# Cross-attention's output projection in two halves of 512 columns, first query groups on token tiles 0 to 3, on one Trainium2 core

## The chip, the cores and the metric

The kernel runs on one core of one Trainium2 chip. The metric is the device time in microseconds (us). The kernel before the change takes 2323.01 us, the median of three runs (2319.06 to 2325.57).

## What is computed

One encoder layer on 1024 tokens of width 1024, all in float32. The reference, cut to the parts that the change lies in:

```python
x = x + concat(A, B) @ W_out              # mixing block, ends just ahead of the change
h = rms_norm(x, norm_xattn_g)
q = (h @ wq)                              # 1024 x 1024, 4 heads of 256
s = q k^T * XATTN_DH ** -0.5              # 256 memory tokens
o = softmax(s) v
x = x + o @ wo                            # output projection
h = rms_norm(x, norm_ffn_g)
logits = h @ router_w + router_b          # 32 experts
top_vals, top_idx = lax.top_k(logits, 4)  # then 4 of 32 experts per token, clamped SwiGLU
```

## The kernel before the change

Tokens lie in 8 tiles of 128 rows, and each 1024-wide contraction in 8 slices of 128. Every engine has its own stream of instructions, written out by hand in order; an engine takes its stream strictly in order, and a semaphore wait at the head of a stream holds all that stands behind it. PE is the matrix engine, DVE the vector engine, ACT the scalar engine, POOL the general one, SP the one that issues most DMAs.

A float32 product is made of three fast products: each operand is split into a high part (a rounded copy, made by ACT) and a low part (the rest, made by DVE by subtraction), and PE adds high x high, high x low and low x high. So each weight chunk of 256 columns, which SP loads into the four-slot buffer `ring`, needs one ACT copy of 128x2048 (`split_wq`, `split_wo`) and one DVE subtraction of 128x2048 (`wq_lo`, `wo_lo`) before PE can use it.

The stages around the change, in order of time:

- **Norm y and query projection (q).** `y_square`, `y_root` (ACT), `y_mean`, `y_scale` (DVE) norm one token tile; `turn_y` (PE) transposes it by eight small matmuls; `hidden_states_hi` (ACT) and `hidden_states_lo` (DVE) split it into `hH` and `hL`. Then 16 groups of 24 matmuls, each 512 tokens wide (tiles 0 to 3, or 4 to 7), four groups for each weight chunk. `turn_y(5)` stands ahead of group 0, `turn_y(6)` ahead of group 1, `turn_y(7)` ahead of group 2.
- **Softmax loop.** 32 steps (4 heads x 8 token tiles) in which PE, DVE and ACT hand each tile on: `score` (PE), `scale_maximum` (DVE), `xprob` (ACT, exponential), `normalise` (DVE), `turn_probabilities` (PE), `xprob_drain` (ACT). From step 10 on, four steps out of eight also hold `head_values` (PE), `xout_hi` (ACT) and `xout_lo` (DVE).
- **Output projection (o).** 32 groups of 24 matmuls, each 256 columns wide: for each of four weight chunks all eight token tiles. DVE adds each group into `xres` (`add_residual`). `woH` and `woL` are two-deep buffers.
- **Norm z and router.** As soon as the last chunk's group of a tile is added, the tile is normed (`z_square`, `z_mean`, `z_root`, `z_scale`), stored, transposed (`turn_z`, PE, 8 small matmuls), copied out (`h3_turned_out`, ACT, two copies). For each pair of tiles `router` (PE) makes partial logits, `logits_out` (ACT) copies them, `sum_groups` (PE) adds the groups up, and DVE takes the best four of 32 (`logits`, `one_hot`). The routing tables follow, then the loop over experts, some three fifths of the time.

Of the kernel before, what the change touches and what calls it, by code (L numbers as in the profile page):

```python
# [25 lines left out]
P = 128  # L26
S = 1024
D = 1024
# [38 lines left out]
def build(nc, A):  # L67

    with ExitStack() as ctx:
# [68 lines left out]
        woH = [sb(f"woH{i}", [P, KT, 256], FR, 96 + 16 * i) for i in range(2)]  # L138
        woL = [sb(f"woL{i}", [P, KT, 256], FR, 104 + 16 * i) for i in range(2)]
# [27 lines left out]
        h3 = sb("h3", [P, TT, D], F, 0)  # L167
# [82 lines left out]
        for n in ("m", "x", "y", "z"):  # L250
# [67 lines left out]

        chunks = ([(w_in, G0), (w_in, A0), (w_in, B0), (w_in, A0 + 256), (w_in, B0 + 256),
# [3 lines left out]
                  + [(wo, 256 * c) for c in range(4)])  # L323
# [3 lines left out]
                + [("out", 8 * (c + 1)) for c in range(4)] + [("q", 4 * (c + 1)) for c in range(4)]  # L327
                + [("o", 8 * (c + 1)) for c in range(4)])
# [93 lines left out]
        def o_bank(n):  # L422
            return PS[:, n % 8 if n < 3 * TT else n % 2, 0:256]
# [38 lines left out]
        def _(sp):  # L462
# [51 lines left out]
            for t in range(TT):  # L514
                sp.wait_ge(norms["z"]["scaled"], t + 1)
                sp.dma_start(h3_dram[P * t:P * (t + 1), :], h3[:, t, :]).then_inc(s_h3s, 16)
# [271 lines left out]
        def _(act):  # L788
# [325 lines left out]
            def split_wq(c):  # L1114

                act.wait_ge(s_ring[slot_of[g_q + c]], 16 * fills[g_q + c])
                if c == 1:
                    act.wait_ge(s_mm["out"], 4 * TT)
                if c >= 2:
                    act.wait_ge(s_mm["q"], 4 * (c - 1))  # L1120
                nc.scalar.copy(wqH[c % 2][:], ring[:, slot_of[g_q + c]]).then_inc(s_dhi, 1)
# [32 lines left out]
            for t in range(TT - 4, TT):  # L1154
                hidden_states_hi(t)
            split_wq(1)
            for n in range(16):
                d = drain("q", n)
                c, ft, th = q_group(n)
                nc.scalar.copy(qxT[:, 2 * c + ft, 512 * th:512 * (th + 1)], bank_groups(n)).then_inc(d, 1)  # L1160
                if n in (3, 7):
                    split_wq(n // 4 + 2)
# [9 lines left out]
            def split_wo(c):  # L1172

                act.wait_ge(s_ring[slot_of[g_o + c]], 16 * fills[g_o + c])
                if c >= 2:
                    act.wait_ge(s_mm["o"], TT * (c - 1))
                nc.scalar.copy(woH[c % 2][:], ring[:, slot_of[g_o + c]]).then_inc(s_dhi, 1)
# [21 lines left out]
            split_wo(1)  # L1199
# [12 lines left out]
            def z_square(t):  # L1212
                act.wait_ge(s_dr["o"], 24 + t + 1)
                if t:
                    act.wait_ge(NZ["stats_by_scalar"], square_of(t - 1))
                nc.scalar.activation(sig[:], xres[:, t, :], ACT.Square,
                                     accum_out=st8[:, 0, t:t + 1]).then_inc(NZ["stats_by_scalar"], 1)

            def z_root(t):
                act.wait_ge(NZ["stats_by_vector"], square_of(t))  # L1220
                nc.scalar.activation(st8[:, 2, t:t + 1], st8[:, 1, t:t + 1], ACT.Sqrt
                                     ).then_inc(NZ["stats_by_scalar"], 1)
# [15 lines left out]
            z_square(0)  # L1238
# [8 lines left out]
            z_root(TT - 1)  # L1247
            h3_turned_out(4)
            logits_out(1)
            h3_turned_out(5)  # L1250
            h3_turned_out(6)
            logits_out(2)
            h3_turned_out(7)
# [239 lines left out]
        def _(dve):  # L1493
# [404 lines left out]
            for c in range(1, 4):  # L1898
                wq_lo(c)
            def wo_lo(c):  # L1900

                dve.wait_ge(s_dhi, N_IN + 8 + c + 1)
                nc.vector.tensor_tensor(woL[c % 2][:], ring[:, slot_of[len(chunks) - 4 + c]], woH[c % 2][:].bitcast(F),
                                        ALU.subtract).then_inc(s_dlv, 1)
# [34 lines left out]
            wo_lo(1)  # L1939
            for n in range(3 * TT):  # L1940
                add_residual("o", n, o_bank)
                if n in (TT - 1, 2 * TT - 1):
                    wo_lo(n // TT + 2)
# [5 lines left out]
            def z_mean(t):  # L1949
                dve.wait_ge(NZ["stats_by_scalar"], square_of(t))  # L1950
                nc.vector.tensor_scalar(st8[:, 1, t:t + 1], st8[:, 0, t:t + 1], 1.0 / D, RMS_EPS, ALU.mult, ALU.add
                                        ).then_inc(NZ["stats_by_vector"], 1)

            def z_scale(t):
                dve.wait_ge(NZ["stats_by_scalar"], root_of(t))
                nc.vector.reciprocal(st8[:, 3, t:t + 1], st8[:, 2, t:t + 1]).then_inc(NZ["stats_by_vector"], 1)
                dve.wait_ge(NZ["stats_by_vector"], root_of(t))
                nc.vector.scalar_tensor_tensor(out=h3[:, t, :], in0=xres[:, t, :], scalar=st8[:, 3, t:t + 1],
                                               in1=gfb[:], op0=ALU.mult, op1=ALU.mult).then_inc(NZ["scaled"], 1)
# [24 lines left out]
            for t in range(TT + 8):  # L1984
                if t < TT:
                    add_residual("o", 3 * TT + t, o_bank)
                if 1 <= t <= TT:
                    z_mean(t - 1)
                if 2 <= t <= TT + 1:
                    z_scale(t - 2)  # L1990
                if 7 <= t <= TT + 6:
                    logits(t - 7)
                if t >= 8:
                    one_hot(t - 8)
# [351 lines left out]
        def _(pe):  # L2346
# [336 lines left out]
            turn_y(5)  # L2683
            pe.wait_ge(NY["drained"], TT)
            for c in range(4):
                pe.wait_ge(s_dlv, c + 1)
                slot = slot_of[g]
                for i in range(4):
                    n = 4 * c + i
                    _, ft, th = q_group(n)  # L2690
                    if n in (1, 2):
                        turn_y(5 + n)
                    if n == 2:
                        pe.wait_ge(NY["drained"], 2 * TT)
                    if n >= 8:
                        pe.wait_ge(s_dr["q"], n - 7)
                    w, rows = slice(P * ft, P * (ft + 1)), slice(512 * th, 512 * (th + 1))
                    for k in range(KT):
                        wh, wl = wqH[c % 2][:, k, w], ringL[:, slot, k, w]
                        xh, xl = hH[:, k, rows], low_of(k)[:, rows]  # L2700
                        pe.matmul(bank_groups(n), wh, xh, start=(k == 0), stop=False)  # L2701
                        pe.matmul(bank_groups(n), wh, xl, start=False, stop=False)
                        ins = pe.matmul(bank_groups(n), wl, xh, start=False, stop=(k == KT - 1))
                    ins.then_inc(s_mm["q"], 1)
                g += 1
# [39 lines left out]
            def turn_z(t):  # L2745
                pe.wait_ge(NZ["scaled"], t + 1)
                if t < 2:
                    pe.wait_ge(s_dr["o"], 3 * TT)
                else:
                    pe.wait_ge(s_h3e, 2 * (t - 1))  # L2750
                for b in range(2):
                    for k in range(4):
                        ins = pe.transpose(PS[:, 4 + 2 * (t % 2) + b, P * k:P * (k + 1)],
                                           h3[:, t, P * (4 * b + k):P * (4 * b + k + 1)], ident[:])
# [24 lines left out]
            for c in range(4):  # L2779
                pe.wait_ge(s_dlv, 4 + c + 1)  # L2780
                for t in range(TT):
                    n = TT * c + t
                    if n >= 8:
                        pe.wait_ge(s_dr["o"], n - 7 if n < 26 else n - 1)
                    tile = slice(P * t, P * (t + 1))
                    for k in range(KT):
# [4 lines left out]
                    if n >= 27:  # L2791
                        turn_z(n - 27)
                    if n == 29:
                        router(0)
                    elif n == 31:
                        sum_groups(0)
                        router(1)

            turn_z(5)
            sum_groups(1)  # L2800
            turn_z(6)
            router(2)
            turn_z(7)
            sum_groups(2)
            router(3)
            sum_groups(3)
            pe.wait_ge(s_dr["o"], 32)
# [212 lines left out]
```

## Time and profile before

| what | value |
|---|---|
| runs of the kernel before, median | 2323.01 us (2319.06, 2323.01, 2325.57) |
| span of the profiled execution | 2318.4 us |
| PE busy | 2181.9 us, 94% of the span |
| DVE busy | 1794.7 us, 77% |
| ACT busy | 1268.4 us, 55% |
| query projection, from PE's first to last matmul | 553.67 to 647.05 us |
| softmax loop | 647.88 to 728.25 us |
| output projection, PE | 728.31 to 825.4 us |
| end of router, first matmul of the routing tables | 843.92 us |
| first expert transposes | 893.99 us |

The profiled execution has no separate time beside its span of 2318.4 us; the fastest of the three runs is 0.7 us above that span and the median 4.6 us. Busy shares are averages over stages: PE is dense in the two projections and in the expert loop, and waits in the softmax loop and around the routing.

### The profile page before, as it was taken

To read this page: it belongs to the slowest core of one execution; us is meant where nothing else is said; L and a number is where in the kernel's file an instruction comes from. 1 tells how busy PE (TensorE), PEld (TensorE's weight loads), DVE (VectorE), ACT (ScalarE), POOL (GpSimd) and SP (SyncE) were. 2 spreads that over 40 slices of the span, in tenths; PEclk is the share of its full clock that TensorE was granted. 3 is DMA by queue.
4 is the path that set the end of the run, shared out by engine and by line. 5 is a ranking of instruction groups with operands and counts; after the bars stand their busy time and mean duration, and the time that the engine had idled before them with its cause. 6 is when DMAs were issued, how large, how long until landed. Compare 5 with 4: busy or idle time off the path is not lost.

```text
span 2318.4 us, 41683 instructions
## 1 busy us (share of the span) xinstructions
PE 2181.9 (94%) x14731; PEld 1742.5 (75%) x14865; DVE 1794.7 (77%) x2020; ACT 1268.4 (55%) x1437; POOL 358.8 (15%) x311
## 2 busy tenths in 40 slices
PE   5999998799989977999999999999999999999995
PEld 4789977698856956777877777777777777877773
DVE  5599989815043376899989898898998989998885
ACT  4422265604142145666766666666666666776554
POOL 0000000020002102222211221122122112221112
PEclk8899999999999988999999999999999999999997
DMA  4211141321101036989988798789788888997777
GB/s 156 72 38 55 37 148 38 125 68 37 55 19 33 10 133 241 385 307 343 402 296 315 292 343 291 278 332 350 295 325 303 300 296 346 397 342 307 278 260 249
DMA packets 113300, 515.58 MB, mean 222 GB/s; under 512 B 11424, under 2 KB 45397, under 8 KB 63714
## 3 DMA queue, kind: packets, MB, share of 16 engines
q1 hardware_dynamic: 97810, 467.28, 52.0%
q0 software_dynamic: 13504, 44.24, 7.9%
q10 hardware_dynamic: 1904, 2.90, 0.5%
q8 instruction: 60, 0.98, 0.2%
q14 instruction: 22, 0.18, 0.0%
HBM read 477.12 MB, written 37.36 MB: 222 GB/s over the span
## 4 chain that ended last, share of the span: by engine, by line
PE 75%; DVE 11%; issue 7%; DMA 4%; ACT 3%; DVEq 0%; POOLq 0%; ACTq 0%; POOL 0%; SPq 0%
PE PS L2901 14%; PE PS L2902 12%; PE PS L2375 10%; PE PS L2904 9%; PE PS L2928 5%; PE PS L2788 4%; PE PS L2630 4%; PE PS L2893 3%; PE PS L2864 2%; DVE wlo L2120 2%; PE PS L2916 1%; ACT whi L1289 1%; DMA raw<-in_exp_w_up 1%; PE PS L2732 1%; PE PS L2701 1%
## 5 line engine op out<-in xcount | busy, mean ns | idle before, releaser
L2120 DVE TENSOR_TENSOR wlo<-raw,whi 128x2048 fp32r<-128x2048 f32 x384 | 869.9, 2287 | 99.7 <-ACT whi L1289 88.9
L1289 ACT CAST whi<-raw 128x2048 fp32r<-128x2048 f32 x384 | 725.2, 1911 | 118.9 <-DMA raw<-in_exp_w_down 55.3
L2901 PE MATMUL PS<-whi,xhi 128*128 128x512 f32 x1024 | 424.2, 414 | 12.7 <-issue 9.3
L2902 PE MATMUL PS<-wlo,xhi 128*128 128x512 f32 x1024 | 400.4, 391 | 0.0
L2904 PE MATMUL PS<-whi,xlo 128*128 128x512 f32 x768 | 301.8, 393 | 0.0
L2902 PEld LDWEIGHTS PS<-wlo,xhi 128*128 128x128 f32 x1024 | 193.3, 189 | 39.9
L2901 PEld LDWEIGHTS PS<-whi,xhi 128*128 128x128 f32 x1024 | 194.2, 190 | 37.8 <-DVE wlo L2120 0.7
L2901 PE MATMUL PS<-whi,hhi 128*128 128x512 f32 x512 | 206.8, 404 | 8.7 <-DVE wlo L2120 5.3
L2902 PE MATMUL PS<-wlo,hhi 128*128 128x512 f32 x512 | 200.6, 392 | 0.0
L2904 PEld LDWEIGHTS PS<-whi,xlo 128*128 128x128 f32 x768 | 144.8, 189 | 31.9
L2904 PE MATMUL PS<-whi,hlo 128*128 128x512 f32 x384 | 150.7, 392 | 0.0
L696 POOL COPY idxc<-TG 128x2 uint32 (+1 forms) x34 | 31.8, 935 | 763.7 <-PE PS L2864 395.6
L1630 DVE SCALAR_TENSOR_TENSOR yT<-u_pad,CWT,yT 128x1024 f32<-128x1024 f32 x120 | 144.3, 1284 | 0.0
L729 POOL DMA_INDIRECT acc_scratch<-yb,idxs x64 | 139.3, 2176 | 22.8 <-issue 22.8
L1347 ACT ACTIVATE yb<-PS,row_gate 128x512 f32<-128x512 f32 x62 | 42.7, 688 | 153.1 <-PE PS L2928 83.5
L2901 PEld LDWEIGHTS PS<-whi,hhi 128*128 128x128 f32 x512 | 96.8, 189 | 39.0 <-issue 10.6
L1338 ACT ACTIVATE sgm<-glu 128x512 f32<-128x512 f32 (+1 forms) x64 | 53.4, 834 | 130.1 <-DVE glu L2165 76.1
L1847 DVE TENSOR_TENSOR xres<-xres,PS 128x256 f32<-128x256 f32 x64 | 26.5, 420 | 125.6 <-PE PS L2788 64.1
L706 POOL DMA_INDIRECT xs<-h_scratch,idxc x68 | 110.5, 1624 | 19.6 <-issue 17.6
L2902 PEld LDWEIGHTS PS<-wlo,hhi 128*128 128x128 f32 x512 | 97.0, 189 | 18.6
L2928 PE MATMUL PS<-raw,xtl 128*32 128x256 f32 x1664 | 103.7, 381 | 0.0
L2893 PE MATMUL PS<-whi,xlo 128*128 128x512 f32 x256 | 99.6, 389 | 0.0
(439 smaller groups left out, 4234.9 us busy)
## 6 DMA issues: line engine op xcount, KB each, us to landing
raw<-in_exp_w_up SPq DMA_DIRECT2D x256, 1024.0 KB, 8.0
raw<-in_exp_w_down SPq DMA_DIRECT2D x128, 1024.0 KB, 7.3
ring<-in_w_in SPq DMA_DIRECT2D x11, 1024.0 KB, 5.8
xres<-in_x SPq DMA_DIRECT2D x4, 1024.0 KB, 10.3
ring<-in_xattn_wk SPq DMA_DIRECT2D x4, 1024.0 KB, 9.2
ring<-in_xattn_wv SPq DMA_DIRECT2D x4, 1024.0 KB, 6.1
ring<-in_w_out SPq DMA_DIRECT2D x4, 1024.0 KB, 12.3
xres<-in_x SPq DMA_DIRECT2D x2, 2048.0 KB, 8.2
```

The lines of the kernel that those rows point to most:

```text
L706: nc.gpsimd.indirect_dma_start(xs[0:rows, b, :], None, h3_dram, bass.IndirectOffsetOnAxis(ap=idxc[0:rows, b:b + 1], axis=0)).then_inc(s_xs ...
L729: nc.gpsimd.indirect_dma_start(acc_dram, bass.IndirectOffsetOnAxis(ap=idxs[0:rows, b:b + 1], axis=0), yb[0:rows, b, :], None, compute_op=A ...
L1289: nc.scalar.copy(whi[:, chunk_slot(c, NSPL), :], raw[chunk_slot(c, NRAW)][:]).then_inc(s_whi, 1)
L1630: ins = nc.vector.scalar_tensor_tensor(out=yT[:, c, :], in0=uc, scalar=w, in1=yT[:, c, :], op0=ALU.mult, op1=ALU.add)
L2120: nc.vector.tensor_tensor(wlo[:, chunk_slot(c, NSPL), :], raw[chunk_slot(c, NRAW)][:], whi[:, chunk_slot(c, NSPL), :].bitcast(F), ALU.subtract
L2375: ins = pe.matmul(out, lhs, rhs, start=(k == 0 and i == 0), stop=(k == KT - 1 and i == 2))
L2630: ins = pe.matmul(out_bank(n), a, b, start=(k == 0 and i == 0 and n >= TT), stop=(k == KT - 1 and i == 2 and n >= TT))
L2893: return pe.matmul(o, lo[:, k, :], whi[:, slot, 3, :], start=False, stop=k == KT - 1)
L2901: pe.matmul(o, hi[:, k, :], wh, start=k == 0 and bias is None, stop=False)
L2902: pe.matmul(o, hi[:, k, :], wl, start=False, stop=False)
L2904: pe.matmul(o, lo[:, k, :], wh, start=False, stop=False)
L2928: ins = pe.matmul(part[2 * (k % 2) + h], tl[:, k, 0:TAIL], chunk[:, k % 4, cols[h]], start=k == 1 or k == 0 and bias is None, stop=k >= KT ...
```

## The change

The diff, cut to its core (SP's list of chunks, buffers, ACT, DVE, PE):

```diff
-        woH = [sb(f"woH{i}", [P, KT, 256], FR, 96 + 16 * i) for i in range(2)]
-        woL = [sb(f"woL{i}", [P, KT, 256], FR, 104 + 16 * i) for i in range(2)]
+        woP = sb("woP", [P, 4, KT, 256], FR, 96)
...
-        h3 = sb("h3", [P, TT, D], F, 0)
+        h3 = [sb("h3a", [P, 2, D], F, 0), sb("h3b", [P, 2, D], F, 24)]
...
+        WO_COLS = (1, 0, 2, 3)
...
         def q_group(n):
-            c, i = n // 4, n % 4
-            ft, th = (i % 2, i // 2) if c == 0 else (i // 2, i % 2)
-            return c, ft, th
+            if n < 8:
+                return n % 4 // 2, n % 2, n // 4
+            return n // 4, n % 4 // 2, n % 2
...
         def o_bank(n):
-            return PS[:, n % 8 if n < 3 * TT else n % 2, 0:256]
+            return PS[:, n if n < TT else n % 2, :]
...ACT, norm y and softmax loop
-            for t in range(TT - 4, TT):
+            hidden_states_hi(TT - 4)
+            split_wq(1)
+            for t in range(TT - 3, TT):
                 hidden_states_hi(t)
-            split_wq(1)
...
                 if 2 <= step < N_SC + 2:
                     xprob_drain(step - 2)
-            split_wo(1)
+                if step == TT:
+                    split_wo(1)
...ACT, norm z
-            for t in range(1, TT):
-                if t >= 4:
-                    h3_turned_out(t - 4)
+            for t in range(TT):
                 z_square(t)
-                z_root(t - 1)
-                if t == 6:
-                    logits_out(0)
+                z_root(t)
+                if t:
+                    h3_turned_out(t - 1)
+                if t in (3, 5, 7):
+                    logits_out((t - 3) // 2)
...DVE
                 if value_part(step - 1):
                     xout_lo(*value_part(step - 1))
-            wo_lo(1)
+                if step == TT:
+                    wo_lo(1)
+
+            def add_attention(n):
+                dve.wait_ge(s_mm["o"], n + 1)
+                xs = xres[:, n % TT, 512 * (n // TT):512 * (n // TT + 1)]
+                nc.vector.tensor_tensor(xs, xs, o_bank(n), ALU.add).then_inc(s_dr["o"], 1)
...
+            for t in range(TT):
+                add_attention(TT + t)
+                if t >= 4:
+                    one_hot(t - 4)
+                z_mean(t)
+                z_scale(t)
+                if t >= 3:
+                    logits(t - 3)
+            one_hot(4)
+            for t in range(5, TT):
+                logits(t)
+                one_hot(t)
...PE
             pe.wait_ge(s_dr["out"], 32)
-            turn_y(5)
             pe.wait_ge(NY["drained"], TT)
...
+                if n == 0:
+                    turn_y(5)
+                    turn_y(6)
+                if n == 1:
+                    turn_y(7)
...
+            for half in range(2):
+                pe.wait_ge(s_dlv, 4 + 2 * (half + 1))
...
                 for t in range(TT):
-                    n = TT * c + t
+                    n = TT * half + t
...
                     for k in range(KT):
-                        for i, (a, b) in enumerate(((oxH, woH), (oxH, woL), (oxL, woH))):
-                            ins = pe.matmul(o_bank(n), a[:, k, tile], b[c % 2][:, k, :],
+                        wh, wl = woP[:, wide, k, :], ringL[:, lows, k, :]
+                        for i, (a, b) in enumerate(((oxH, wh), (oxH, wl), (oxL, wh))):
+                            ins = pe.matmul(o, a[:, k, tile], b,
                                             start=(k == 0 and i == 0), stop=(k == KT - 1 and i == 2))
+                        if half and t in (3, 5, 7) and k == 3:
+                            router((t - 3) // 2)
                     ins.then_inc(s_mm["o"], 1)
...
+                    if half and t:
+                        turn_z(t - 1)
+                    if half and t in (3, 5, 7):
+                        sum_groups((t - 3) // 2)
+
+            turn_z(TT - 1)
             router(3)
             sum_groups(3)
```

What it does. The query projection's first four groups take both first weight chunks on tiles 0 to 3, so chunk 1 is split earlier and the transposes of tiles 5 to 7 stand behind groups 0 and 1. The output projection runs as 16 groups of 24 matmuls of 512 columns; each matmul's moving operand is two blocks of 256 columns that lie apart in memory. Chunks 0 and 1 must both be split ahead of its first group, and chunk 1's split moves into step 8 of the softmax loop. The add into `xres` is 512 wide. In the second half each tile is complete after its one group, and its norm, transpose and router work stand between the groups.

On PE, around the first group of the query projection, names as before (`XNy` is the normed tile, L2659 `turn_y`, L2701 to L2703 the three products). Before:

```order
L2659 MATMUL PS<-ident,XNy_105 128x128 x8
L2659 MATMUL PS<-ident,XNy_106 128x128 x8
L2701 MATMUL PS<-hH,wqH_107 128x512
L2702 MATMUL PS<-hL_102,wqH_107 128x512
L2703 MATMUL PS<-hH,ringL 128x512
```

After:

```order
L2672 MATMUL PS<-ident,XNy_105 128x128 x8
L2709 MATMUL PS<-hH,wqH_107 128x512
L2710 MATMUL PS<-hL_102,wqH_107 128x512
L2711 MATMUL PS<-hH,ringL 128x512
```

The second transpose (tile 5) no longer stands ahead of the first product; it comes 24 matmuls later, with that of tile 6 right behind it.

On ACT, steps 7 to 9 of the softmax loop (`pr` the probabilities, `pT` the transposed ones), after the change:

```order
L1190 ACTIVATE pr,smx<-PS,smx 128x256
L1175 COPY pT<-PS 128x2x128
L1183 CAST woP<-ring 128x2048
L1190 ACTIVATE pr,smx<-PS,smx 128x256
L1175 COPY pT<-PS 128x2x128
```

The CAST is `split_wo(1)`; before, it stood behind the whole loop, after the last `oxH`. DVE has the matching subtraction (`ringL<-ring,woP`) at the same step, behind `normalise(7)` and ahead of `scale_maximum(9)`.

On PE, the end of the fourth group of the second half (`h3b` the normed tile, L2766 `turn_z`, L2787 `sum_groups`, L2805 the projection), after the change:

```order
L2805 MATMUL PS<-ringL,oxH 128x512
L2805 MATMUL PS<-woP,oxL 128x512
L2766 MATMUL PS<-ident,h3b 128x128 x8
L2787 MATMUL PS<-stack,lgs 128x32 x2
L2805 MATMUL PS<-woP,oxH 128x512
```

and on ACT the rows of the same tile, the square and root of tile 3 first, then tile 2's two copies and the logits' copy that `sum_groups(0)` reads:

```order
L1223 ACTIVATE sig,st_120<-xres 128x1024
L1228 ACTIVATE st_120<-st_120 128x1
L1236 COPY h3T<-PS 128x512 x2
L1243 COPY lgs<-PS 128x256
```

Before, `sum_groups(0)` stood behind the last group of the projection, eight tiles on; now it stands three groups after the first tile is complete, and again so for the second and third pair.

## Rows read from the trace of the kernel before

**Rows 1.** The page, the chain that ended last, by engine.

```profile
PE 75%; DVE 11%; issue 7%; DMA 4%; ACT 3%; DVEq 0%; POOLq 0%; ACTq 0%; POOL 0%; SPq 0%
```

**Rows 2.** Timeline of PE, query projection (start, duration, instruction, [idle before]).

```profile
553.67 1.39 PE L2659 MATMUL PS<-ident,XNy 128*128 128x128 f32 x8 [2.45 <-DVE hL L1882]
...
570.74 0.50 PE L2701 MATMUL PS<-hH,wqH 128*128 128x512 f32 x1 [1.68 <-DVE hL L1882]
...
571.54 0.40 PE L2701 MATMUL PS<-hH,wqH 128*128 128x512 f32 x1
...
646.82 0.39 PE L2703 MATMUL PS<-hH,ringL 128*128 128x512 f32 x1
```

**Rows 3.** The chain that ended last, 545 to 560 us (start, time in chain).

```profile
557.19 0.43 PE PS L2703
...
557.93 0.23 PE PS L2702
```

**Rows 4.** Timeline of all engines, softmax steps 8 to 10.

```profile
664.53 0.36 ACT L1167 COPY pT<-PS 128x256 f32<-128x256 f32 x1
...
664.94 0.42 DVE L1928 TENSOR_REDUCE smx<-PS 128x1 f32<-128x256 f32 x1 [0.44 <-PE PS L2712]
...
665.28 1.03 PE L2712 MATMUL PS<-kx,qxT 128*128 128x256 f32 x4
...
666.47 1.98 PE L2732 MATMUL PS<-pT,vx 128*128 128x512 f32 x4 [0.15 <-ACT pT L1167]
```

**Rows 5.** Timeline, end of the softmax loop and first group of o.

```profile
727.43 1.90 ACT L1177 CAST woH<-ring 128x2048 fp32r<-128x2048 f32 x1
...
728.31 0.39 PE L2788 MATMUL PS<-woH,oxH 128*128 128x256 f32 x1 [1.40 <-DVE oxL L1910]
...
729.36 2.29 DVE L1903 TENSOR_TENSOR woL<-ring,woH 128x2048 fp32r<-128x2048 f32 x1 [1.11 <-ACT woH L1177]
```

**Rows 6.** The chain that ended last, groups of o with transposes and router between.

```profile
810.08 2.87 PE PS L2788 x24
812.95 0.87 PE PS L2753 x8
...
817.57 1.00 PE PS L2766 x16
818.57 3.07 PE PS L2788 x24
```

**Rows 7.** Timeline, norm z of the last tile and a sum of logits.

```profile
825.41 0.42 DVE L1847 TENSOR_TENSOR xres<-xres,PS 128x256 f32<-128x256 f32 x1 [1.86 <-PE PS L2788]
...
825.87 1.06 ACT L1216 ACTIVATE sig<-xres 128x1024 f32<-128x1024 f32 x1 [1.26 <-DVE xres L1847]
...
826.83 0.19 ACT L1216 ACTIVATION_READ_ACCUMULATOR sig<-xres 128x1 f32 x1
...
828.01 0.20 ACT L1221 ACTIVATE st<-st 128x1 f32<-128x1 f32 x1 [0.89 <-DVE st L1951]
...
829.49 0.63 PE L2774 MATMUL PS<-stack,lgs 128*128 128x32 f32 x4 [0.85 <-ACT lgs L1236]
```

**Rows 8.** Timeline, from the last transpose to the routing tables.

```profile
832.32 1.09 PE L2753 MATMUL PS<-ident,h 128*128 128x128 f32 x8 [0.29 <-DVE h L1958]
...
835.20 0.18 DVE L1964 TENSOR_TENSOR LG<-PS,rbb 128x32 f32<-128x32 f32 x1
...
835.70 0.63 PE L2774 MATMUL PS<-stack,lgs 128*128 128x32 f32 x4 [0.49 <-ACT lgs L1236]
...
836.71 0.18 DVE L1964 TENSOR_TENSOR LG<-PS,rbb 128x32 f32<-128x32 f32 x1
836.74 2.33 POOL L691 TENSOR_TENSOR bdn<-bdn,bdn 32x1024 fp32r<-32x1024 f32 x1 [73.30 <-ACT bdn L1257]
...
837.34 1.76 DVE L1972 CAST IXf<-IX 128x8 f32<-128x8 uint32 x1
...
843.92 0.21 PE L2813 MATMUL PS<-Mb,beforeb 128*128 128x32 bf16 x2 [7.59 <-issue]
```

More of the change, by code:

```diff
@@ L322, in build @@
                   + [(w_out, 256 * c) for c in range(4)] + [(wq, 256 * c) for c in range(4)]
-                  + [(wo, 256 * c) for c in range(4)])
+                  + [(wo, 256 * c) for c in WO_COLS])
         used = ([("in", n) for n in (2, 14, 18, 22, 26, 30, 34, 42, 50, 62, 70)]
                 + [("mem", 2 * (c + 1)) for c in range(8)]
-                + [("out", 8 * (c + 1)) for c in range(4)] + [("q", 4 * (c + 1)) for c in range(4)]
-                + [("o", 8 * (c + 1)) for c in range(4)])
+                + [("out", 8 * (c + 1)) for c in range(4)] + [("q", n) for n in (6, 8, 12, 16)]
+                + [("o", 8), ("o", 8), ("o", 16), ("o", 16)])
         N_IN, g_out = 11, 19
@@ L422, in o_bank, with z_square_count, z_root_count @@
         def o_bank(n):
-            return PS[:, n % 8 if n < 3 * TT else n % 2, 0:256]
+            return PS[:, n if n < TT else n % 2, :]
+        def z_square_count(t):
+            return 2 * t + 1
+        def z_root_count(t):
+            return 2 * t + 2
         GM, ZB, CB, LG_, LB, NG = 0, 8, 12, 16, 20, 24
@@ L1174, in split_wo @@
                 act.wait_ge(s_ring[slot_of[g_o + c]], 16 * fills[g_o + c])
-                if c >= 2:
-                    act.wait_ge(s_mm["o"], TT * (c - 1))
-                nc.scalar.copy(woH[c % 2][:], ring[:, slot_of[g_o + c]]).then_inc(s_dhi, 1)
+                nc.scalar.copy(woP[:, WO_COLS[c]], ring[:, slot_of[g_o + c]]).then_inc(s_dhi, 1)
             split_wo(0)
@@ L1897, in _ @@
                     hidden_states_lo(t - 4)
-            for c in range(1, 4):
+                if t == TT:
+                    wq_lo(1)
+            for c in range(2, 4):
                 wq_lo(c)
@@ L1938, in _ @@
                     xout_lo(*value_part(step - 1))
-            wo_lo(1)
[L1940 to L1943, printed above, removed]
+                if step == TT:
[4 more added lines that the diff above has]
+                nc.vector.tensor_tensor(xs, xs, o_bank(n), ALU.add).then_inc(s_dr["o"], 1)
+            for n in range(TT):
+                add_attention(n)
+                if n in (1, 3):
+                    wo_lo(n // 2 + 2)
             NZ = norms["z"]
@@ L1954, in z_scale @@
             def z_scale(t):
-                dve.wait_ge(NZ["stats_by_scalar"], root_of(t))
+                dve.wait_ge(NZ["stats_by_scalar"], z_root_count(t))
                 nc.vector.reciprocal(st8[:, 3, t:t + 1], st8[:, 2, t:t + 1]).then_inc(NZ["stats_by_vector"], 1)
-                dve.wait_ge(NZ["stats_by_vector"], root_of(t))
-                nc.vector.scalar_tensor_tensor(out=h3[:, t, :], in0=xres[:, t, :], scalar=st8[:, 3, t:t + 1],
+                dve.wait_ge(NZ["stats_by_vector"], z_root_count(t))
+                if t >= 4:
+                    dve.wait_ge(s_h3s, 16 * t)
+                    dve.wait_ge(NZ["turned"], 2 * (t - 3))
+                nc.vector.scalar_tensor_tensor(out=h3_of(t), in0=xres[:, t, :], scalar=st8[:, 3, t:t + 1],
                                                in1=gfb[:], op0=ALU.mult, op1=ALU.mult).then_inc(NZ["scaled"], 1)
@@ L1982, in one_hot @@
                                         ).then_inc(s_hot, 1)
[L1984 to L1994, printed above, removed]
+            for t in range(TT):
+                add_attention(TT + t)
+                if t >= 4:
+                    one_hot(t - 4)
[7 more added lines that the diff above has]
+                one_hot(t)
             dve.wait_ge(s_hot, 4 * TT)
@@ L2682, in _ @@
             pe.wait_ge(s_dr["out"], 32)
-            turn_y(5)
             pe.wait_ge(NY["drained"], TT)
-            for c in range(4):
+            for n in range(16):
+                c, ft, th = q_group(n)
                 pe.wait_ge(s_dlv, c + 1)
[L2687 to L2705, printed above, removed]
+                slot = slot_of[g + c]
+                if n == 4:
+                    pe.wait_ge(NY["drained"], 2 * TT)
+                if n >= 8:
+                    pe.wait_ge(s_dr["q"], n - 7)
+                w, rows = slice(P * ft, P * (ft + 1)), slice(512 * th, 512 * (th + 1))
+                for k in range(KT):
+                    wh, wl = wqH[c % 2][:, k, w], ringL[:, slot, k, w]
+                    xh, xl = hH[:, k, rows], low_of(k)[:, rows]
+                    pe.matmul(bank_groups(n), wh, xh, start=(k == 0), stop=False)
+                    pe.matmul(bank_groups(n), wh, xl, start=False, stop=False)
+                    ins = pe.matmul(bank_groups(n), wl, xh, start=False, stop=(k == KT - 1))
+                ins.then_inc(s_mm["q"], 1)
+                if n == 0:
[3 more added lines that the diff above has]
+                    turn_y(7)
+            g += 4
             pe.wait_ge(s_dr["q"], 16)
@@ L2747, in turn_z @@
                 if t < 2:
-                    pe.wait_ge(s_dr["o"], 3 * TT)
+                    pe.wait_ge(s_dr["o"], TT)
                 else:
@@ L2778, in _ @@
             pe.wait_ge(s_axl, 16)
-            for c in range(4):
-                pe.wait_ge(s_dlv, 4 + c + 1)
+            for half in range(2):
+                pe.wait_ge(s_dlv, 4 + 2 * (half + 1))
+                lows = slice(0, 4, 3) if half == 0 else slice(1, 3)
+                wide = slice(2 * half, 2 * half + 2)
                 for t in range(TT):
-                    n = TT * c + t
+                    n = TT * half + t
                     if n >= 8:
-                        pe.wait_ge(s_dr["o"], n - 7 if n < 26 else n - 1)
+                        pe.wait_ge(s_dr["o"], n - 7 if n < 10 else n - 1)
                     tile = slice(P * t, P * (t + 1))
+                    o = o_bank(n).rearrange("p (c n) -> p c n", c=2)
                     for k in range(KT):
-                        for i, (a, b) in enumerate(((oxH, woH), (oxH, woL), (oxL, woH))):
-                            ins = pe.matmul(o_bank(n), a[:, k, tile], b[c % 2][:, k, :],
+                        wh, wl = woP[:, wide, k, :], ringL[:, lows, k, :]
+                        for i, (a, b) in enumerate(((oxH, wh), (oxH, wl), (oxL, wh))):
+                            ins = pe.matmul(o, a[:, k, tile], b,
                                             start=(k == 0 and i == 0), stop=(k == KT - 1 and i == 2))
+                        if half and t in (3, 5, 7) and k == 3:
+                            router((t - 3) // 2)
                     ins.then_inc(s_mm["o"], 1)
[L2791 to L2804, printed above, removed]
+                    if half and t:
[3 more added lines that the diff above has]
+            turn_z(TT - 1)
             router(3)
             sum_groups(3)
-            pe.wait_ge(s_dr["o"], 32)
+            pe.wait_ge(s_dr["o"], 2 * TT)
             pe.wait_ge(s_hot, 4 * TT)
```

31 lines of the change are left out of this document (13 added, 18 removed).

## The prediction

> **What bounds the kernel now.** I read the chain of work that ended last first: three quarters of it is PE, a tenth DVE [rows 1]. The two projections that the change touches are PE from end to end, so there a matmul saved is time saved. Between them lies the softmax loop, in which each step passes through PE, DVE and ACT in turn, and behind them the router, where PE waits for ACT and DVE, and the chain runs through DVE's picks. Everything behind the router (routing tables, gather, expert loop) starts from its end, so a shift of that end is a shift of the whole. I read the timeline for four places and ask of each what waits last. Times are from the one profiled execution, span 2318.4 us; the sum is a difference, and I put it on the runs' median of 2323.0, which is 4.6 above that span.
>
> **Query projection.** Now PE waits twice: 2.45 us ahead of `turn_y(5)`, for tile 3's low part, and 1.68 us ahead of group 2, for tile 7's [rows 2]. The first wait stays: group 0 needs the same low part. The second goes, because groups 0 to 3 need tiles 0 to 3 only, and tile 7's low part, late by 1.7 us today, now has two more groups (11 us) to get ready. Chunk 1's split is one ACT copy of 1.9 and one DVE subtraction of 2.3 us, behind tile 4's copies; it is done some 6 us after PE starts, and group 2 asks for it at 15 us. It pushes tile 7's scaling by under 3 us, which `turn_y(7)` (14 us in) doesn't feel. The sum: 332 matmuls from 571.54 to 646.82 are 0.2267 us each [rows 2], so a group is 5.44. After the first wait PE's matmuls start 0.43 us apart up to 557.6 and 0.23 after it [rows 3]: the clock is at 1.2 GHz for some 3.7 us after PE stood idle for 2.45, and at 2.4 GHz after 1.68 idle. The stage is 384 x 0.2267 = 87.05, three transposes at 0.87 = 2.6, and about 1.7 of half clock = 91.4, against 93.4 now (553.67 to 646.82 + 0.23). **Minus 2.0 us.**
>
> **Softmax loop.** Today chunk 1's split runs 727.43 to 731.65, behind the loop, while PE already works on chunk 0 [rows 5]: it costs nothing. Now it stands in step 8. ACT does it after the copy that ends at 664.89 [rows 4], for 1.9 us; DVE can't begin before that copy is done, and stands still until then; it subtracts for 2.3 us. So `scale_maximum(9)`, at 664.94 today, starts at 664.8 + 1.93 + 2.2 = 668.95, 4.0 us late. Behind it on ACT are `xprob(9)` and `xprob_drain(7)`, and `head_values` (666.47 today) waits for that drain. PE can run ahead by score 10 only (ends 666.31 [rows 4]) and then stands idle some 4.2 us. Nothing gives this back: the steps that follow are PE's own. Bounds: 0 if the loop had slack, 4.2 if all of both instructions counts. I take 4.0. On top, 4.2 us idle is more than the 2.45 that halved the clock, and the next steps, with `head_values`, are bound by PE: some 3.5 us at half clock, as behind the first wait of the query projection [rows 3], lose 1.6. **Plus 5.6 us.**
>
> **Output projection up to its last group.** Two 256-wide matmuls take 2 x 2.87 / 24 = 0.239 us [rows 6], one 512-wide 0.2267 [rows 2]. The q groups read a moving operand in one piece; here it is two pieces of 256, which no row shows. Bounds: 0.2267 (no price) and 0.239 (all of the gain lost), 5 us apart over 384 matmuls. I take the low one, since the pieces are long. The Trainium skill, "TensorE: Matmul & The Clock Gate", section "Back-to-back issue gap", gives N/2.4 + 2.5 ns at full clock, by which pairs of 256 lose just 2.5 ns against a 512, 1.0 us in all where the rows give 5.0; the measured pitch of both shapes is above it, so the rows decide.
> From the first matmul (728.31) to where DVE can start on the last group: 97.1 today (825.41 [rows 7]). Then: 16 x 5.44 + 0.2 = 87.2; six `turn_z` at 0.87 = 5.2; three routers at 1.0 + 0.2 [rows 6] = 3.6; two `sum_groups` at 0.5 (each lasts 0.63 [rows 7], the next instruction starts a little before its end) = 1.0. That would be 97.0, no change. But the `sum_groups` wait. Let T be the moment DVE starts on tile 3. Its add is twice as wide as the 0.42 of today [rows 7]: between that and 0.84, I take 0.7. ACT's square starts at T + 0.73 and its sum is out 1.15 later (825.87 to 826.83 + 0.19 [rows 7]), T + 1.88; mean on DVE, 0.15 and two hand-overs, root starts T + 2.10. Only then come tile 2's two copies and the logits' copy, since ACT works in order: from root to PE's sum is 829.49 - 828.01 = 1.48 [rows 7], so T + 3.58. PE has finished issuing `turn_z(2)` at T + 0.65. It stands for **2.9 us**, and every later group is behind it. The same at the second pair: 5.9 in two. Its idle time by the record is 2.6 us each, above the 2.45 that halved the clock and well above the 1.68 that didn't: 1.6 each, 3.2. So 97.1 becomes 97.0 + 5.9 + 3.2 = 106.1. **Plus 9.0 us.** The new waits of `z_scale` for stored tiles cost nothing: a store lands 3 us after its issue and a group and a half lie between.
>
> **The tail.** Today 18.5 us from 825.41 to 843.92 [rows 7, 8]: four tiles of norm and all of the picks are still to do. After the change only tile 7's norm and four tiles' picks are. PE's third sum at T + 3.58, `turn_z(7)` at T + 4.1, the last sum 3.38 behind it (832.32 to 835.70 [rows 8]), T + 7.5, DVE's picks from T + 8.1. Picks for a tile are 1.51 (835.20 to 836.71 [rows 8]); two tiles hang on the last sum: T + 11.2. POOL's 2.33 us operation stops DVE's copy for 1.6 today (1.76 instead of 0.15 [rows 8]); it starts 1.04 after the last sum there and here, so it still hits: up to 1.9, T + 13.1. The third wait of 2.6 us leaves the transposes and the router at half clock: 1.0 more. 14.1 against 18.5. **Minus 4.4 us.**
>
> **Sum:** -2.0 + 5.6 + 9.0 - 4.4 = +8.2, and 2323.0 + 8.2 = 2331.
>
> **Rivals.** (0.3% is 7 us, about what a measurement of this kernel tells from no change.)
> (a) *The clock holds.* The short waits don't lower it: for it, 1.68 us idle did nothing; against it, 2.45 did. Then -3.2 in the projection, -1.0 in the tail, -1.6 in the softmax loop: 8.2 - 5.8 = +2.4, 2325, not slower by this measure. It decides from the point where two of the four drops fail to come.
> (b) *The two pieces cost.* A 512-wide matmul on two blocks goes at the pace of two 256-wide ones, or worse: +5, 2336. For it, no row has this shape; against it, each piece is 1 KB long. By the pitch that the Trainium skill gives, 4 us less would be saved than by my rows, near 2335.
> (c) *The logits' copy is not late.* If PE didn't wait for it, the projection would cost 97.0 and the tail 13.1: -2.0 + 5.6 - 0.1 - 5.4 = -1.9, 2321. Against it: ACT's order has the copy behind tile 3's root, and the root behind DVE's add of the very group that PE has just ended. It would take ACT records out of that order.
> (d) *The split in step 8 is hidden*, with the rest as forecast: +8.2 - 5.6 = +2.6, 2325.6. Against it, DVE and ACT wait for each other under 0.5 us a step [rows 4].
>
> **How the numbers follow.** Forecast (all four terms within 3 us in sum) 0.52; (a) 0.18; (b) 0.15; (c) 0.08; (d) 0.07. Of the forecast's own range, 2327 to 2335, some six tenths are above +7. So slower by over 0.3%: 0.52 x 0.62 + 0.15 + a little of (a) = 0.50; within it 0.39, from the rest of the forecast, (a), (d) and most of (c); faster 0.11, since the runs themselves differ by 6 us and the stages behind may fall differently. The range from (c) to beyond (b): 2321 to 2338.
>
> **What the profile after would show.** In the query projection one PE wait of some 2.5 us and none ahead of group 2. In step 9 of the softmax loop an idle PE of about 4 us, released by the transposed probabilities' copy, and half-clock matmuls behind it. In the second half PE idle some 2.6 us ahead of each `sum_groups`, released by ACT's `lgs` copy, and matmuls 0.43 apart behind it. From the last add to the routing tables 13 to 14 us. Matmuls of 512 columns 0.227 apart. The prediction is wrong if PE's records show no such waits, or if the shape's pitch is not near 0.227.

## The result, and the profile after

The changed kernel takes 2329.82 us, the median of 14 runs (2322.64 to 2334.18), beside 2320.63 us for the kernel before, again 14 runs. The ratio is 1.0037, 95% interval 1.0029 to 1.0046: 8.6 us slower. The forecast was +8.2 us and 2331. The difference is worked out from the ratio; the two medians lie 9.2 us apart. The profiled execution of the changed kernel has a span of 2330.7 us and is one of the slower of its 14 (2332.46 us), so the two profiles lie 12.3 us apart, 3.7 more than the timing says.

The page after, the same line as [rows 1], the chain of work that ended last by engine:

```profile
PE 81%; DVE 8%; issue 6%; ACT 3%; DMA 2%; POOLq 0%; DVEq 0%; POOL 0%; SPq 0%; ACTq 0%
```

PE has a larger share of the chain, though it has fewer matmuls than before. The timeline of PE in the query projection, answering to [rows 2]:

```profile
554.09 0.47 PE L2709 MATMUL PS<-hH,wqH 128*128 128x512 f32 x1 [2.40 <-issue]
554.39 0.40 PE L2710 MATMUL PS<-hL,wqH 128*128 128x512 f32 x1
...
559.62 1.91 PE L2672 MATMUL PS<-ident,XNy 128*128 128x128 f32 x16
561.28 0.48 PE L2709 MATMUL PS<-hH,wqH 128*128 128x512 f32 x1
...
643.68 0.39 PE L2711 MATMUL PS<-hH,ringL 128*128 128x512 f32 x1
```

One wait is left, at the head, and none ahead of group 2: the stage runs from 554.09 to 643.91, 89.8 us where it was 93.4. The first row says "issue" for what ended the wait, so this view doesn't name the releaser. Behind the 2.40 us of idling the matmuls go at full pitch at once, 24 of them in 5.53 us (554.09 to 559.62), and the granted clock of the stretch 554 to 559 us is 1.00 (the mean over a stretch, where 1.00 is 2.4 GHz and 0.50 is 1.2 GHz); in the kernel before it is 0.66 there, behind 2.45 us of idling [rows 2, 3].

The timeline in the softmax loop, steps 8 to 10, answering to [rows 4]:

```profile
658.93 0.42 DVE L1930 TENSOR_REDUCE smx<-PS 128x1 f32<-128x256 f32 x1 [0.47 <-PE PS L2725]
...
660.32 0.42 DVE L1930 TENSOR_REDUCE smx<-PS 128x1 f32<-128x256 f32 x1 [0.32 <-PE PS L2725]
...
661.68 1.91 ACT L1183 CAST woP<-ring 128x2048 fp32r<-128x2048 f32 x1
...
663.62 2.29 DVE L1905 TENSOR_TENSOR ringL<-ring,woP 128x2048 fp32r<-128x2048 f32 x1 [2.24 <-ACT woP L1183]
665.83 0.42 DVE L1930 TENSOR_REDUCE smx<-PS 128x1 f32<-128x256 f32 x1
...
667.35 3.78 PE L2745 MATMUL PS<-pT,vx 128*128 128x512 f32 x4 [4.14 <-ACT pT L1175]
...
672.69 1.88 PE L2745 MATMUL PS<-pT,vx 128*128 128x512 f32 x4
```

DVE's maxima (L1930) start 1.4 to 1.55 us apart up to 660.32, and the next one only 5.51 us later, at 665.83: DVE stands 2.24 us until ACT's split is done, subtracts, and only then takes it. PE idles 4.14 us, and the first four matmuls of `head_values` then take 3.78 us instead of 1.98. The stage, from the last matmul of q to the first of o, is 88.9 us instead of 81.3, and its mean granted clock 0.90 instead of 0.96.

The chain that ended last, second half of the output projection, answering to [rows 6, 7]:

```profile
732.79 54.70 PE PS L2805 x240
787.49 0.87 PE PS L2766 x8
788.36 5.47 PE PS L2805 x24
...
798.44 3.00 PE PS L2805 x12
801.45 0.02 issue
801.47 0.70 DVE xres L1947
802.17 0.02 issue
802.19 1.16 ACT sig L1223 x2
...
803.67 1.05 ACT h3T L1236 x2
804.72 0.28 ACT lgs L1243
805.01 0.04 issue
805.05 0.75 PE PS L2787 x4
805.80 7.05 PE PS L2805 x24
...
824.73 7.18 PE PS L2805 x24
```

Read it downwards: a group ends, DVE adds, ACT squares, copies the previous tile, copies the logits, and only then PE sums them and goes on. The chain has left PE for 3.6 us. The group behind it takes 7.05 us and the one behind the second sum 7.18, where the group at 788.36, with no wait ahead of it, takes 5.47. The granted clock of the stretches 805 to 813 and 824 to 832 us is 0.79 in both. From 732.79 to the DVE add of the last group (839.58 us) it is 106.8 us, instead of 97.1.

The tail, the same view:

```profile
843.15 1.06 PE PS L2787 x4
844.22 1.77 PE PS L2766 x8
...
846.65 1.98 PE PS L2779 x16
848.63 0.02 issue
848.65 0.38 ACT lgs L1243
849.03 0.04 issue
849.07 1.08 PE PS L2787 x4
...
850.92 1.52 DVE IXf L1984
```

The last transposes take 1.77 and the router 1.98 us, both at half clock (0.87 and 1.00 in [rows 6]; the granted clock from 843 to 850 us is 0.50), and POOL still stops one DVE copy (1.52). From the last add to the first matmul of the routing tables (855.02 us) it is 15.4 us instead of 18.5. The five pieces: query -3.6, softmax +7.6, projection +9.7, tail -3.1, and +1.6 outside the stages that the change touches (0.4 ahead of the query projection, 1.2 behind the first matmul of the routing tables), together 12.3.

### The profile page after: what moved, and what is told of

The parts are those of the page before. It is cut to its first block, busy times and chain, and to the rows that moved or that the text cites. A ratio compares the mean times of both kernels' runs of the same rounds, so it can differ in the third digit from the quotient of the medians.

```text
span 2330.7 us, 41039 instructions
## 1 busy us (share of the span) xinstructions
PE 2191.7 (94%) x14480; PEld 1727.4 (74%) x14481; DVE 1795.6 (77%) x2004; ACT 1268.5 (54%) x1437; POOL 353.1 (15%) x311
## 4 chain that ended last, share of the span: by engine, by line
PE 81%; DVE 8%; issue 6%; ACT 3%; DMA 2%; POOLq 0%; DVEq 0%; POOL 0%; SPq 0%; ACTq 0%
PE PS L2912 14%; PE PS L2913 13%; PE PS L2388 10%; PE PS L2915 10%; PE PS L2939 5%; PE PS L2643 4%; PE PS L2805 4%; PE PS L2904 3%; PE PS L2875 2%; PE PS L2927 1%; PE PS L2958 1%; PE PS L2745 1%; PE PS L2709 1%; PE PS L2711 1%; PE PS L2710 1%
## 5 line engine op out<-in xcount | busy, mean ns | idle before, releaser
L2133 DVE TENSOR_TENSOR wlo<-raw,whi 128x2048 fp32r<-128x2048 f32 x384 | 869.8, 2286 | 100.1 <-ACT whi L1288 88.9
L2912 PEld LDWEIGHTS PS<-whi,hhi 128*128 128x128 f32 x512 | 96.8, 189 | 38.6 <-issue 10.8
L2913 PEld LDWEIGHTS PS<-wlo,hhi 128*128 128x128 f32 x512 | 96.9, 189 | 18.5
L713 POOL DMA_INDIRECT xs<-h_scratch,idxc x68 | 106.8, 1571 | 20.0 <-issue 18.2
L663 POOL TENSOR_TENSOR ringL<-ring,wuH 128x2048 fp32r<-128x2048 f32 x3 | 13.8, 4614 | 490.7 <-ACT wuH L982 490.7
## 6 DMA issues: line engine op xcount, KB each, us to landing
ring<-in_w_out SPq DMA_DIRECT2D x4, 1024.0 KB, 12.3
```

The costliest lines, as they stand in the source:

```text
L713: nc.gpsimd.indirect_dma_start(xs[0:rows, b, :], None, h3_dram, bass.IndirectOffsetOnAxis(ap=idxc[0:rows, b:b + 1], axis=0)).then_inc(s_xs ...
L2133: nc.vector.tensor_tensor(wlo[:, chunk_slot(c, NSPL), :], raw[chunk_slot(c, NRAW)][:], whi[:, chunk_slot(c, NSPL), :].bitcast(F), ALU.subtract
L2912: pe.matmul(o, hi[:, k, :], wh, start=k == 0 and bias is None, stop=False)
L2913: pe.matmul(o, hi[:, k, :], wl, start=False, stop=False)
```

## The experiments

In all of them the ratio is to the kernel before, on the same chip; 0.001 is 2.3 us, and differences in us are worked out from ratios. The interval of one ratio is some 2 to 3 us either way, so that of a difference between two experiments is 3 to 4 us either way. Stage lengths are from each profile: q from its first to its last matmul's start, softmax from there to the start of o, o to its last matmul's start, the tail to the routing tables. By that measure the kernel before has 92.1, 81.5, 96.8 and 18.8 us, the changed one 89.6, 89.1, 106.4 and 15.9.

**The copy of the logits first.** Of the changed kernel, ACT's order alone:

```diff
             for t in range(TT):
+                if t in (3, 5, 7):
+                    logits_out((t - 3) // 2)
                 z_square(t)
                 z_root(t)
                 if t:
                     h3_turned_out(t - 1)
-                if t in (3, 5, 7):
-                    logits_out((t - 3) // 2)
```

> The changed kernel with one move on ACT: the copy of the logits that sum_groups waits for stands ahead of the tile's square and root, not behind the previous tile's copies. Theory (the sum of logits waits for that copy): PE's two waits of 2.7 us ahead of the sums go, the half clock behind them goes, and the third wait in the tail too: 5.5 + 3 + 1 to 1.5, so 9 to 10 us less than the changed kernel, about 1 us under the kernel before. Rival (the two-piece moving operand or the 512-wide adds cost the time of this stage): no more than 1 us less than the changed kernel. Rival (the waits move, PE waits for something else there): less than 4 us less.

Ratio 0.9996 (0.9987 to 1.0005), 2319.7 us: 9.5 us below the changed kernel, as the theory had it. The stage o is 97.2 us, 9.2 less than in the changed kernel, and the tail 14.4, 1.5 less; the softmax loop is as long as there (89.3). The chain of that kernel at the first sum:

```profile
799.20 2.99 PE PS L2805 x12
802.19 0.87 PE PS L2766 x8
803.07 0.37 PE PS L2787 x4
803.43 2.62 PE PS L2805 x11
```

The sum follows the transposes without a gap. No operation was taken away, so shapes and adds are not the cause of this stage's loss, and the place of one 0.39 us copy is. The 9.2 us add up: two waits of 2.74 us, 3.1 of half clock in the two groups behind them (7.05 and 7.18 us, here 5.58 each), and 0.6 in the two sums (0.75 and 0.63, here 0.37 each).

**The split at the end of the loop.** Of the changed kernel, the step of ACT's split and DVE's subtraction:

```diff
-                if step == TT:
+                if step == N_SC + 1:
                     split_wo(1)
...
-                if step == TT:
+                if step == N_SC + 1:
                     wo_lo(1)
```

> The changed kernel with chunk 1's split (ACT copy, DVE subtraction) moved from step 8 of the softmax loop to step 33, where ACT and DVE stand for 3.9 and 6.3 us while PE multiplies the last head's values. Theory (the split in step 8 stalls the loop by its two durations, and the clock falls behind the stall): the loop is 4.0 us shorter and 1.6 to 3.6 us of half clock go, 5.6 to 7.6 us less than the changed kernel; the loop's end is not later, since 4.2 us of split fit in 6.3. Rival (the loop had slack, and the 7.6 us that this stage is longer come from elsewhere): no change, or up to 3 us more if the split is exposed at the end.

Ratio 1.0042 (1.0028 to 1.0057), 2328.5 us: no gain, a miss. Yet its profile has a softmax stage of 80.4 us, 8.7 less than the changed kernel's, and a stage o of 109.3, 2.9 more. Its timeline at the loop's end shows that the split is covered, DVE being done with it just as the first head output is due:

```profile
717.39 2.29 DVE L1905 TENSOR_TENSOR ringL<-ring,woP 128x2048 fp32r<-128x2048 f32 x1 [3.43 <-ACT woP L1183]
719.16 0.58 ACT L1195 CAST oxH<-PS 128x512 fp32r<-128x512 f32 x1 [1.81 <-PE PS L2745]
719.78 0.69 DVE L1912 TENSOR_TENSOR oxL<-PS,oxH 128x512 fp32r<-128x512 f32 x1
```

and its chain shows where a part of the gain went, in the groups behind the sums:

```profile
798.11 1.06 PE PS L2787 x4
799.18 8.21 PE PS L2805 x24
```

8.21 us (and 8.17 behind the second) instead of 7.05 and 7.18, and 1.06 for each sum instead of 0.75 and 0.63: the same wait was followed by a longer stretch at half clock. The granted clock from 798 to 807 us is 0.63.

**Both moves.**

> Both moves together: logits' copy first and the split at step 33. If the two causes are separate and account for the loss, the sum of the two single gains, 15 to 17 us less than the changed kernel: about 6 to 8 us under the kernel before, ratio 0.997. If they overlap or one wait replaces another, less than 12 us under the changed kernel.

Ratio 0.9977 (0.9968 to 0.9987), 2313.7 us. The profile: softmax 80.4, o 97.2, tail 14.4. This beats both kernels, by 5.3 us against the one before and some 14 against the changed one. That is less than the 15 to 17 that were expected, but as much as the two moves gave one by one if the split's is taken from its second timing below (9.5 and 4.4).

**The query part alone**, on the kernel before: `q_group`, the place of `split_wq` and `wq_lo(1)`, and PE's loop of groups as in the change, nothing else.

> The kernel before with the query part of the change alone (first four groups on token tiles 0 to 3, chunk 1 split earlier, late transposes between). Theory: PE's wait of 1.7 to 1.9 us ahead of group 2 goes and nothing else moves: 2.0 us under the kernel before, 3.5 us if the clock holds behind the first wait as it did in the changed kernel's profile. Rival (the earlier split delays the late tiles and the gain is eaten): within 0.5 us of the kernel before.

Ratio 0.9992 (0.9982 to 1.0002), 2316.8 us, 1.9 us less and not clear of the noise. The profile has 91.2 us for q instead of 92.1 between starts of matmuls (the transposes of tile 5 stood ahead of the first one before, 1.0 more), with the half clock at its head; o and the tail are as before (96.8 and 18.8). The softmax loop, in which no instruction was changed, is 80.0 us instead of 81.5, with a mean granted clock of 0.98 instead of 0.96: this stage differs by 1.5 us without any stall.

**Extra transposes in the waits.** Of the changed kernel, PE's stream ahead of the first two sums:

```diff
+                    if half and t in (3, 5):
+                        pe.wait_ge(s_dr["o"], n)
+                        for _ in range(24):
+                            pe.transpose(PS[:, (n + 1) % 2, 0:P], ident[:], ident[:])
                     if half and t in (3, 5, 7):
                         sum_groups((t - 3) // 2)
```

> The changed kernel with 24 extra transposes of a constant ahead of each of the first two sums of logits, into a bank that the next group clears: they take 2.6 us, about the length of PE's wait there, and nothing waits for them. Theory (part of the price is the half clock behind the wait): the waits' length stays, the matmuls behind them keep a pitch of 0.228 us, 3 to 5.5 us less than the changed kernel. Rival (the wait is all there is, the clock would hold): no change, or up to 0.6 us more.

Ratio 1.0037 (1.0024 to 1.0050) from five runs. The stage o is 103.2 us, 3.2 less, and the chain behind the first two sums:

```profile
801.20 5.58 PE PS L2805 x24
...
818.65 5.58 PE PS L2805 x24
```

So the sum still waits, PE's idling ahead of it is filled, and the half clock behind it is gone: 5.58 us, not 7.05, with a granted clock of 1.00 from 800.5 to 807 us. The timing doesn't show the 3 us, a miss; with five runs its interval is 6 us wide. The profiled execution is the fastest of the five. Its softmax loop is 84.4 us with a mean granted clock of 0.98, though every instruction up to the loop's end is the changed kernel's, which took 89.1 at 0.90, and the stall of 4.14 us is there as well. So the half clock that goes with the stall isn't fixed by the loop's instructions.

**The changed kernel again**, unaltered.

> The changed kernel once more, unaltered, beside the next one on the same chip: ratio 1.0037, with its own profile. If the price of the half clock depends on where the waits fall, the groups behind the two sums take other than 7.05 and 7.18 us this time; with a fixed price they take the same.

Ratio 1.0042 (1.0030 to 1.0054). Its stages are those of the first profile to 0.1 us (89.6, 89.1, 106.4, 15.9), and the two groups behind the sums take 7.04 and 7.18. The half clock's price was the same in both profiles of this kernel.

**The split at the loop's end again**, on the same chip as the last.

> The kernel of the split at step 33 once more, unaltered, on the same chip as the changed kernel. By the profiles its softmax loop is 8.8 us shorter, by the first timing it is no faster. Theory A (the loop's gain is real and partly given back by dearer half clocks behind the sums of logits, 2.7 instead of 1.6 us each): 3 to 6 us less than the changed kernel here. Theory B (the stall in the softmax loop costs little in ordinary runs): within 1.5 us of it.

Ratio 1.0023 (1.0013 to 1.0034), 0.0019 or 4.4 us below the changed kernel beside it. Its chain:

```profile
801.11 1.06 PE PS L2787 x4
802.17 8.16 PE PS L2805 x24
...
821.58 1.06 PE PS L2787 x4
822.64 8.16 PE PS L2805 x24
```

8.16 twice, beside 8.21 and 8.17 in the first run of this kernel, although everything from the query projection on falls 3.0 us later in this profile. The softmax stage is 80.4 (8.7 less) and o 109.2 (2.8 more): 5.9 less by the profile, which the 4.4 agree with. That fits theory A of the expectation; taken alone it is only just clear of noise (0.7 to 8 us by the two intervals), and the first timing of this kernel was 4 us higher than this one.

**The split at the end and the extra transposes.**

> The split at step 33 together with the extra transposes ahead of the first two sums, so that no half clock follows them and the softmax loop's gain can't be given back there. Theory A: 5.6 to 8.8 us less than the kernel with the transposes alone. Theory B: within 1.5 us of it.

Ratio 0.9999 (0.9989 to 1.0009), 8.8 us below the kernel with the transposes alone and 5.6 below that with the split at the end. That is theory A again. Softmax 80.0, o 103.1, tail 14.7. Beside the profile of the kernel with the transposes alone the loop is 4.4 us shorter, at the same mean clock of 0.98: this is the stall without any difference in half clock. The timing gave twice as much. The profiled execution of the kernel with the transposes alone is 5 us below its median, and if its loop took 89 us in the other four the 8.8 would be explained; no profile shows that.

**Both moves and extra transposes** in PE's two remaining waits, 22 ahead of query group 0 and 24 ahead of the last tile's transposes.

> The two moves together (logits' copy first, split at step 33) with extra transposes of a constant in PE's two remaining waits of some 2.5 us: 22 ahead of query group 0, 24 ahead of the last tile's transposes. If the clock price of those waits is theirs, the query stage always takes 89.6 instead of mostly 91.2 us, and the tail from the projection's last matmul to the routing tables 13 instead of 14.4: 1.5 to 3 us less than the two moves alone. If the extra work is in the way, or the clock holds anyway, no less.

Ratio 0.9963 (0.9951 to 0.9976), 2311.1 us, the fastest of all; q takes 89.6 us, the tail 13.6. In this profile the softmax loop is 81.4, 0.9 to 1.4 more than with both moves alone, which gives back a part.

**Both moves again**, beside it.

> The two moves together once more, unaltered, on the same chip as the one with the extra transposes: ratio 0.997 to 0.998 to the kernel before, that is 5 to 7 us less.

Ratio 0.9977 (0.9967 to 0.9986), 2313.7 us, as the first time. The extra transposes are worth 3 us (0.0014) here, but the two intervals overlap.

## Why the prediction was right, point by point

**Query projection, -2.0.** The wait ahead of group 2 went, as forecast, and nothing was late behind it. The profile shows -3.6: the half clock of some 1.7 us at the stage's head did not come this time, though the wait there was 2.40 us instead of 2.45. It isn't a matter of that 0.05: all ten experiments have this order, and of the nine whose wait is not filled eight have a stage of 91.2 us behind an equal wait (2.40 or 2.41 us) and one, the changed kernel run again, 89.6. So the forecast described the usual case. The query part by itself took 1.9 us less by its timing, not clear of noise, and 1.9 by its profile (91.2 instead of 92.1 and the 1.0 of tile 5's transposes).

**Softmax loop, +5.6.** The stall is the 4.0 us that were added up: `head_values` starts 23.4 us after the stage's start, 19.4 before. The half clock was reckoned at 1.6 and cost 3.6 in this profile: 2.4 in the first value step, right behind the stall, and 1.2 at the loop's end, some 50 us later, mostly in the last 16 matmuls of `head_values` (9.74 us of the chain instead of 8.83). These 16 take 7.15 us in four of the experiments' profiles, one of them with the stall, so the 1.2 isn't shown to come from it. Moving the split away gave 8.7 to 8.9 us in the pairs of profiles where the clock differs too, and 4.4 in the pair with equal clock; by timing it gave 4.4 (twice, with the logits' copy late and with it first) and 8.8, and the first comparison, with nothing, stands against it. The term as forecast, 5.6, lies between.

**Projection, +9.0.** Measured 9.7. The two waits were forecast at T + 3.58 for the sum, and the record has it at 805.05 with T at 801.47: T + 3.58. PE's idle time there is 2.74 us in each, where 2.6 was forecast. The half clock cost 1.5 and 1.6 in the groups behind them (beside 5.58 us at full clock) and 0.1 in the first sum, together the 3.2 of the forecast. The copy's move alone gave back 9.2 of this stage and 1.5 in the tail.

**Two pieces of 256 (rival b).** Refuted by 168 matmuls of the first half, which stand between these two rows of PE's timeline after the change:

```profile
738.36 0.39 PE L2805 MATMUL PS<-woP,oxH 128*128 128x512 f32 x1
...
776.44 0.39 PE L2805 MATMUL PS<-woP,oxH 128*128 128x512 f32 x1
```

They are seven groups of 24 and take 38.08 us, 0.2267 each, which is what the one-piece matmuls of q have [rows 2]: the second piece costs nothing here. The Trainium skill, "TensorE: Matmul & The Clock Gate", section "Back-to-back issue gap", gives N/2.4 + 2.5 ns for a single matmul by itself, 215.8 ns for 512 columns, and about 131 ns for 512 columns in a stream of pairs of a weight load and a matmul. The trace agrees with neither, with 226.7 ns here and 119.6 for a 256-wide one [rows 6], where each is paired with a load of weights, and the measurement decides.

**Tail, -4.4.** The order was right, the size off: -3.1. From the third sum on everything on PE ran at half clock, the last transposes, the router and the last sum taking 1.77, 1.98 and 1.08 us, 2.3 us more in the last three alone instead of the 1.0 that was allowed. POOL's operation hit as forecast (1.55 us for a copy of 0.15).

**The rivals.** (a), the clock holds: it did at the head of the query projection, in both profiles of this kernel, and fell at each of the four other waits. (c), the logits' copy not late: its own condition was built as an experiment, and gave 0.9 us less than the kernel before where the rival said 1.9 less. (d), the split hidden: not so, PE stood 4.14 us behind it.

**How near the sum came, and why.** By timing the change costs 8.6 us where 8.2 was forecast. The mechanism is the forecast one in all four places, but that the two numbers lie 0.4 apart is partly luck: the terms are off by -1.6, +2.0, +0.7 and +1.3, the touched stages of the profile add up to some +10.7, and the interval of the timing alone is 2 us either way.

What stays open: why the half clock behind the same 2.74 us wait costs 1.5 to 1.6 us in one kernel and 2.6 in another, to a tenth the same each time. The order of PE's work around the waits is the same in both. When they fall, counted from the span's start, doesn't decide it: the other kernel's first wait ends at 798.11 us in one profile and 801.11 in the other. Nor do the instructions ahead of a wait: the kernels built from the changed one, but for the one that is filled there, have the same ones up to the query projection; the changed one itself takes 89.6 us there and the others 91.2. The 1.6 us outside the touched stages also have no cause shown. Between the profiles of all these kernels the start of the query projection differs by 4.8 us (552.45 to 557.21) and the stretch behind the first matmul of the routing tables by 2.5, and nothing was changed in either; so a difference of a few us between two whole profiles says nothing, and stages have to be compared.

## What to carry to other kernels

Where an engine takes its work in order, look at what stands ahead of the small operation that a dense engine waits for: here a copy of 0.39 us, whose input had been ready 6 us earlier (the router's matmuls begin at 797.44 and take 1.0 us, the copy begins at 804.61), stood behind the next tile's norm and stopped PE for 2.7 us three times. A wait in a dense stretch of PE can cost more than its length, since the matmuls behind it may run at half clock; so remove it if the order allows, and else try to fill it. Filling was worth 1, 3 and 6 us in three comparisons, of which only the last is clear of noise. And when work is moved ahead of time so that something may start earlier, find the place where both of its engines stand still anyway; 25 steps on it was covered.

## What the runs showed of the hardware that was not expected

Behind PE's waits of 2.40 to 2.74 us the clock is not a matter of the wait's length alone: behind one of 2.40 or 2.41 us at the head of the query projection the stage was 91.2 us long in eight profiles and 89.6 in the two of the changed kernel, and behind 2.74 the next group lost 1.5 to 1.6 us in both profiles of one kernel and 2.6 us in both of another. The softmax loop of the changed kernel, with the same instructions, took 89.1 to 89.3 us at a mean granted clock of 0.90 in three profiles and 84.4 us at 0.98 in a fourth. Transposes of a constant, with no use for the result, held the clock at 2.4 GHz through such a wait: the granted clock stayed at 1.00 and the next 24 matmuls took 5.58 us instead of 7.05 to 8.21. A matmul whose moving operand is two blocks of 256 columns that lie apart took 0.2267 us, as one with a single block of 512.
